# A two-block transformer kernel on one core: bias table in parts, one strip split on VectorE, a maximum moved ahead of a gate, and a reordered first stage

## The reference, cut to what matters

```python
def reference(x, ...):
    x = first_block(...)          # norm, projections, windowed attention, spatial gating, conv-gated MLP
    return second_block(x, ...)   # 16 meta tokens put in front

# second_block, after norm and projection
y_mla = _mla(...) * silu(g_mla)   # 8 latent heads, softmax over all 528 positions
y_na  = _na(...)  * silu(g_na)    # 16 heads, neighbourhood attention on an 8 x 64 grid + meta keys
h_res = h_res + concat([y_mla, y_na]) @ w_out
return h_res[:, 16:]
# in _na: s_win = q.k * scale + bias[head, dr, dc];  s_meta = q.k_meta * scale + meta_bias[head]
```

## Time and profile before

| | |
|---|---|
| median of 3 runs | 1300.63 us (1299.13 to 1302.37) |
| profiled execution | 1300.07 us |
| its span | 1298.3 us |
| TensorE busy | 98% of the span |
| VectorE, ScalarE, GpSimd busy | 57%, 36%, 48% |
| granted TensorE clock, mean | 0.998 of full speed |

### The profile page before, as it was taken

How to read it: one execution, slowest core, us unless ns; L and a number is a source line. 1 busy time by engine, 2 the same in 40 slices (tenths; PEclk the granted TensorE clock), 3 DMA queues, 4 the chain that set the end, 5 groups by cost and what they waited for, 6 DMA issues and landing times.

```text
span 1298.3 us, 20151 instructions
## 1 busy us (share of the span) xinstructions
PE 1267.6 (98%) x6814; PEld 1037.6 (80%) x6814; DVE 735.0 (57%) x1402; ACT 470.8 (36%) x1027; POOL 624.4 (48%) x416
## 2 busy tenths in 40 slices
PE   7999999999999999999999999999999999999998
PEld 6877777778788888888888878888878788888877
DVE  5236777567874545442324778778643556666532
ACT  3233333412422222221113556566402454555521
POOL 5433233237454444345563153443347777777712
PEclk9999999999999999999999999999999999999999
DMA  6412222233242333323333211111133322222213
GB/s 180 119 46 85 81 65 72 60 98 97 75 120 84 95 95 96 98 78 101 98 97 98 66 50 49 48 32 49 49 96 93 94 78 78 77 77 77 65 33 98
DMA packets 196755, 105.42 MB, mean 81 GB/s; under 512 B 19174, under 2 KB 194636, under 8 KB 196700
## 3 DMA queue, kind: packets, MB, share of 16 engines
q1 hardware_dynamic: 196252, 104.00, 28.3%
q0 software_dynamic: 432, 0.69, 0.3%
q10 hardware_dynamic: 16, 0.00, 0.0%
HBM read 102.57 MB, written 2.10 MB: 81 GB/s over the span
## 4 chain that ended last, share of the span: by engine, by line
PE 84%; DVE 5%; POOL 4%; issue 2%; ACT 2%; DMA 2%; SPq 1%; DVEq 0%; ACTq 0%; POOLq 0%
PE ps L387 20%; PE ps L388 19%; PE ps L389 19%; PE ps L418 7%; POOL w_low L366 2%; POOL nb L760 2%; PE ps L1397 1%; PE ps L1428 1%; PE ps L1157 1%; PE ps L1408 1%; DVE w_high L361 1%; PE ps L400 1%; PE ps L401 1%; PE ps L404 1%; DMA x_tok<-in_x_dram 1%
## 5 line engine op out<-in xcount | busy, mean ns | idle before, releaser
L366 POOL TENSOR_TENSOR w_low<-w_raw,w_high 128x1024 fp32r<-128x1024 f32 x180 | 440.3, 2448 | 475.2 <-DVE w_high L361 470.0
L387 PE MATMUL ps<-h_high,w_high 128*128 128x512 f32 x816 | 331.2, 406 | 0.9 <-DVE h_low L527 0.4
L388 PE MATMUL ps<-h_low,w_high 128*128 128x512 f32 x816 | 322.3, 395 | 0.0
L389 PE MATMUL ps<-h_high,w_low 128*128 128x512 f32 x816 | 321.1, 394 | 0.0
L361 DVE CAST w_high<-w_raw 128x1024 fp32r<-128x1024 f32 x183 | 150.1, 822 | 115.6 <-DMA w_raw<-in_w_in_dram 44.0
L387 PEld LDWEIGHTS ps<-h_high,w_high 128*128 128x128 f32 x816 | 153.3, 188 | 40.4 <-issue 5.4
L389 PEld LDWEIGHTS ps<-h_high,w_low 128*128 128x128 f32 x816 | 153.4, 188 | 34.9
L388 PEld LDWEIGHTS ps<-h_low,w_high 128*128 128x128 f32 x816 | 153.3, 188 | 33.8 <-issue 2.6
L1713 ACT ACTIVATE z<-ps,cv 128x512 f32<-128x512 f32 x42 | 32.7, 778 | 147.4 <-PE ps L389 147.4
L2315 DVE SCALAR_TENSOR_TENSOR z<-ps,cv,z 128x511 f32<-128x511 f32 x42 | 31.4, 749 | 91.9 <-ACT z L1713 91.9
L389 PE MATMUL ps<-m_high,w_low 128*128 128x512 f32 x176 | 69.4, 395 | 0.0
(11 more groups left out here) (374 smaller groups left out, 2382.2 us busy)
## 6 DMA issues: line engine op xcount, KB each, us to landing
w_raw<-in_w_in_dram SPq DMA_DIRECT2D x150, 256.0 KB, 3.2
w_raw<-in_w_up_dram SPq DMA_DIRECT2D x88, 256.0 KB, 3.1
w_raw<-in_w_out_dram SPq DMA_DIRECT2D x44, 256.0 KB, 3.0
w_raw<-in_w_down_dram SPq DMA_DIRECT2D x32, 256.0 KB, 3.0
w_raw<-in_w_down_dram SPq DMA_DIRECT2D x16, 192.0 KB, 2.6
rel<-in_rel_bias_dram SPq DMA_DIRECT2D x16, 192.0 KB, 3.0
x_tok<-in_x_dram SPq DMA_DIRECT2D x4, 512.0 KB, 5.5
w_raw<-in_w_ob_dram SPq DMA_DIRECT2D x8, 256.0 KB, 2.9
```

What stands on the lines that cost most here:

```text
L366: pool.tensor_tensor(w_low[:, n % RING, :], w_raw[:, n % RAW, :], w_high[:, n % RING, :].bitcast(F32), ALU.subtract).then_inc(low_made, 1)
L387: pe.matmul(acc, wh, mh, start=first and k == 0, stop=False)
L388: pe.matmul(acc, wh, ml, start=False, stop=False)
L389: done = pe.matmul(acc, wl, mh, start=False, stop=last and k == tiles - 1)
```

## The change

Five things are changed.

1. First stage. SP issues token tile 0 first, then the identity, then tile 2; ACT issues tiles 1 and 3 and after them `rows_m`. Tiles 1 and 3 are squared on VectorE, 0 and 2 on ACT; ACT scales tile 3 and keeps raw tile 0. TensorE's turns of the scaled tiles are put in an order that needs fewer banks at first. VectorE's order is: gain copy, square 1, scale 0 and 1, square 3, scale 2, keep raw 1, `make_high(0)`.
2. First strip. TensorE waits for strip 0's high half only, multiplies by it for all k, and follows with the low weights three k later; the six k are done before the raw turns of tiles 2 and 3, as they were.
3. Latent attention. `m_top(0, 0, 0)` is ahead of `m_gate(0, 0)` and `make_high(N_MLA + 4)`; TensorE's wait for the split of the rotary key is inside the first scores, ahead of the products that use it.
4. Pair 1's bias table in three parts on GpSimd: head 0 between `make_low(N_NA + 6)` and `make_low(N_NA + 7)`; head 1 after `make_low(N_NA + 8)`; the four meta copies after `low_of(.., 1)`.
5. Last stage. Strip `N_ON + 4` is split on VectorE (`split_here`); tile 2's second half of the output is stored by ACT.

```diff
 @block.sync
-            sp.dma_start(ident[:], c_ident).then_inc(s["ident_in"], 16)
-            for t in range(4):
-                sp.dma_start(x_tok[:, t, :], ...)
+            sp.dma_start(x_tok[:, 0, :], x[0, 0:P, :]).then_inc(s["x_in"], 16)
+            sp.dma_start(ident[:], c_ident).then_inc(s["ident_in"], 16)
+            sp.dma_start(x_tok[:, 2, :], x[0, 2 * P:3 * P, :]).then_inc(s["x_rest_in"], 16)
...
                 for t in range(4):
+                    if (half, t) == (1, 2):
+                        continue
 @block.gpsimd
-            def bias_table(i, c):
+            def bias_table(i, c, hs=(0, 1), meta=True):
...
             def pair(i, c, more=True):
                 if more:
                     ahead = N_NA + 4 * (c + 2)
                     if c:
                         bias_table(i, c + 1)
                     squares_low(i, c + 1, 0)
                     make_low(pool, ahead, i * 8)
+                    if c == 0:
+                        bias_table(i, 1, (1,), False)
                 if c:
                     y_parts(i, c - 1)
                 if more:
                     squares_low(i, c + 1, 1)
-                    if c == 0:
-                        bias_table(i, c + 1)
                     make_low(pool, ahead + 1, i * 8)
                     low_of(i, c + 1, 0)
                     low_of(i, c + 1, 1)
+                    if c == 0:
+                        bias_table(i, 1, ())
                     make_low(pool, ahead + 2, i * 8)
                     make_low(pool, ahead + 3, i * 8)
...
-            for n in range(N_NA + 5, N_NA + 8):
+            for n in range(N_NA + 5, N_NA + 7):
                 make_low(pool, n)
+            bias_table(0, 1, (0,), False)
+            make_low(pool, N_NA + 7)
             pair(0, 0)
...
-            for n in range(N_ON + 4, N_END):
+            for n in range(N_ON + 5, N_END):
 @block.tensor
+            pe.wait_ge(s["norm_scaled"], 2)
+            for k in range(4):
+                row_turn(0, k)
+            pe.wait_ge(s["x_ready"], 1)
+            for k in range(4, 6):
+                row_turn(0, k)
+            pe.wait_ge(s["norm_scaled"], 4)
+            for k in range(6):
+                row_turn(1, k)
             pe.wait_ge(s["x_ready"], 2)
-            ... (all turns, after both x_ready)
-            pe.wait_ge(low_made, 1)
-            product(pe, ps[:, 0, :], N_SGU, 0, P, KT, hx, ks=(0, 6), ready=("norm_low", 0))
+            for k in range(6, KT):
+                row_turn(0, k)
+                row_turn(1, k)
+            pe.wait_ge(high_made, 1)
+            for k in range(6 + 3):
+                if k < 6:
+                    pe.wait_ge(s["norm_low"], k + 1)
+                    wh, (mh, ml) = w_high[:, 0, k * P:(k + 1) * P], hx(k)
+                    pe.matmul(ps[:, 0, :], wh, mh, start=k == 0, stop=False)
+                    pe.matmul(ps[:, 0, :], wh, ml, start=False, stop=False)
+                if k >= 3:
+                    if k == 3:
+                        pe.wait_ge(low_made, 1)
+                    pe.matmul(ps[:, 0, :], w_low[:, 0, (k - 3) * P:(k - 2) * P], hx(k - 3)[0], start=False, stop=False)
...
+                    if first and b == 0:
+                        pe.wait_ge(s["pe_split"], 2)
...
-            pe.wait_ge(s["pe_split"], 2)
             m_scores(0, 0, 0, first=True)
 @block.scalar
+            act.dma_start(x_tok[:, 1, :], x[0, P:2 * P, :]).then_inc(s["x_in"], 16)
+            act.dma_start(x_tok[:, 3, :], x[0, 3 * P:S, :]).then_inc(s["x_rest_in"], 16)
             act.dma_start(rows_m[:], mix_norm[0].rearrange("(c p) -> c p", p=P)).then_inc(s["consts_in"], 16)
...
+                if half == 0:
+                    raw_copy(0, 4, 2)
+            act.wait_ge(s["norm_root"], 4)
+            act.activation(xh_tok[:, 3, :], x_tok[:, 3, :], ACT.Copy, scale=x_root[:, 3:4]).then_inc(s["norm_scaled"], 1)
...
+            act.wait_ge(s["out_left"], 6)
+            act.dma_start(out[0]...[2][:, :, 512:D], y_tok[:, 2, 512:D]).then_inc(s["out_stored"], 16)
 @block.vector
-            keep_x(0, 4, 2)
+            square_token(1, s["x_in"])
+            scaled_tokens(0, (0, 1))
+            square_token(3, s["x_rest_in"])
+            scaled_tokens(1, (2,))
             keep_x(1, 6, 3)
-            scaled_tokens(0)
-            scaled_tokens(1)
             make_high(dve, 0)
...
                 m_top(i, c, 0)
+                if c == 0:
+                    m_gate(0, 0)
+                    make_high(dve, N_MLA + 4)
...
             m_place_v(0, 0)
-            m_gate(0, 0)
-            make_high(dve, N_MLA + 4)
             head_then_odd(0, 0)
...
-                make_high(dve, N_ON + m + 4)
+                if m == 0:
+                    split_here(dve, N_ON + 4)
+                else:
+                    make_high(dve, N_ON + m + 4)
```

More of the change, by code:

```diff
@@ L749, in bias_table @@
                 z_ = c % 2
-                for h in range(2):
+                for h in hs:
                     for o, m, r, n in ((NA_OFF[1] + META, 8, 8, 2), (NA_OFF[1] + META + P, P + 8, P + 8, 2),
@@ L761, in bias_table @@
                             .then_inc(s["nb_ready"], 1)
-                for o in (0, NA_OFF[1], NA_OFF[2] + 2 * P, NA_OFF[3] + P):
+                for o in (0, NA_OFF[1], NA_OFF[2] + 2 * P, NA_OFF[3] + P) if meta else ():
                     pool.tensor_copy(nb[:, z_, :, o:o + META],
@@ L846, in _, with row_turn @@
             raw_turn(1, 6)
-            pe.wait_ge(s["x_ready"], 2)
[L848 to L854, removed]
-            pe.wait_ge(low_made, 1)
-            product(pe, ps[:, 0, :], N_SGU, 0, P, KT, hx, ks=(0, 6), ready=("norm_low", 0))
+            def row_turn(half, k):
+                for t in (2 * half, 2 * half + 1):
+                    mm = pe.transpose(ps[:, k, t * P:(t + 1) * P], xh_tok[:, t, k * P:(k + 1) * P], ident[:])
+                if half:
+                    mm.then_inc(s["in_turned"], 1)
+            pe.wait_ge(s["norm_scaled"], 2)
[7 more added lines that the diff above has]
+                row_turn(1, k)
+            pe.wait_ge(s["x_ready"], 2)
+            for k in range(6, KT):
[12 more added lines that the diff above has]
+                    pe.matmul(ps[:, 0, :], w_low[:, 0, (k - 3) * P:(k - 2) * P], hx(k - 3)[0], start=False, stop=False)
             pe.wait_ge(s["x_rest_in"], 32)
@@ L1579, in _, with raw_copy @@
             act.wait_ge(s["ones_set"], 2)
+            def raw_copy(t, bank, count):
+                act.wait_ge(s["in_turned"], count)
+                act.activation(x_t[:, :, t * P:(t + 1) * P],
+                               ps[:, bank:bank + 2, :].rearrange("p b (k q) -> p (b k) q", q=P), ACT.Copy)\
+                    .then_inc(s["x_ready"], 1)
             for half in range(2):
+                t = 2 * half
                 act.wait_ge(s[("x_in", "x_rest_in")[half]], 32)
-                for t in (2 * half, 2 * half + 1):
-                    act.activation(xh_tok[:, t, :], x_tok[:, t, :], ACT.Square, accum_out=x_sum[:, t:t + 1])\
-                        .then_inc(s["norm_sq"], 1)
+                act.activation(xh_tok[:, t, :], x_tok[:, t, :], ACT.Square, accum_out=x_sum[:, t:t + 1])\
+                    .then_inc(s["norm_sq"], 1)
                 act.wait_ge(s["norm_sq"], 2 * half + 2)
@@ L2086, in _ @@
                 act.activation(y_tok[:, t, 512:D], ps[:, OUT_BANK[t], :], ACT.Copy).then_inc(s["out_left"], 1)
+            act.wait_ge(s["out_left"], 6)
+            act.dma_start(out[0].rearrange("(r g c) d -> g c r d", g=CG, c=16)[2][:, :, 512:D], y_tok[:, 2, 512:D])\
+                .then_inc(s["out_stored"], 16)
         @block.vector
@@ L2093, in _, with scaled_tokens @@
             dve.tensor_copy(mix_gain[:], ps[:, 4, 0:KT]).then_inc(s["cols_ready"], 1)
-            def scaled_tokens(half):
+            def scaled_tokens(half, ts):
                 dve.wait_ge(s["norm_root"], 2 * half + 2)
-                for t in (2 * half, 2 * half + 1):
+                for t in ts:
                     dve.tensor_scalar(xh_tok[:, t, :], x_tok[:, t, :], x_root[:, t:t + 1], None, ALU.mult)\
@@ L2104, in keep_x, with square_token @@
                                 ps[:, bank:bank + 2, :].rearrange("p b (k q) -> p (b k) q", q=P)).then_inc(s["x_ready"], 1)
-            keep_x(0, 4, 2)
+            def square_token(t, ready):
+                dve.wait_ge(ready, 32)
+                dve.tensor_tensor_reduce(xh_tok[:, t, :], x_tok[:, t, :], x_tok[:, t, :], 1.0, 0.0, ALU.mult, ALU.add,
+                                         x_sum[:, t:t + 1]).then_inc(s["norm_sq"], 1)
+            square_token(1, s["x_in"])
+            scaled_tokens(0, (0, 1))
+            square_token(3, s["x_rest_in"])
+            scaled_tokens(1, (2,))
             keep_x(1, 6, 3)
-            scaled_tokens(0)
-            scaled_tokens(1)
             make_high(dve, 0)
```

1 line of the change is left out of this document (removed).

## The result

The changed kernel took 1303.12 us (median of 20 runs, 1301.54 to 1304.47), the kernel before 1300.07 in as many runs beside it: ratio 1.0019, 95% interval 1.0012 to 1.0026, or +2.5 us. That is slower by something real, and inside the 0.3% that the prediction called no change. 1303.1 had been predicted.

A forecast was written before the change was run, and what follows sets the result against it. TensorE was taken as the bound, busy 98% of the span, so only its idle places could give time back. The terms +1.1 + 0 + 3.5 - 1.2 - 0.4 = +3.0 on 1300.07 gave 1303.1 us, range 1296.0 to 1305.6.

The forecast's parts named there:

- `rows_m` (R = 9.7, chain of 8.2, +0.4): First stage: `rows_m` lands at R, VectorE's chain takes 8.2 us from there, so the first `h_low` starts 0.4 later.
- Starting by the high half alone is worth nothing.: First product: no gain from starting without the low half, since `h_low` and not `w_low` comes last.
- The 0.7 of the lag: First product: low weights three k behind leave three more matmuls after the sixth `h_low`, costing 0.7 us.
- Latent attention 0: Second scores' 1.8 us wait goes but is waited a few instructions later: gain 0, from -0.2 to +0.2.
- one of the signs: Latent attention: no wait for `me` at the second scores, but some 1.8 us at L1217 to L1220 or the turn before.
- the squares that the prediction named: Latent attention: GpSimd's `m_squares`, behind `make_low(N_MLA + 4)`, were to be what TensorE waits for next.
- The table: +3.5 from 1.9 (table's end) and 1.6 (exclusion): Pair 1's bias table: later end costs 1.9 net, filled GpSimd gaps delaying VectorE 1.6; range +1.9 to +4.3.
- The 21.6 us chain: From pair 1's table end through strip `N_NA + 10` to TensorE going on: 21.6 us, with no free time.
- The exclusion: Pair 0: GpSimd instructions in the filled gaps hold up VectorE's `probs` and `normed`; 1.6 us, between nothing and 2.4.
- Last stage: -1.2 and -0.4: VectorE's low half of strip `N_ON + 4` saves 1.2 of 1.71 us; last store on its own queue saves 0.4.
- The table in the gaps does what it says: Rival, pair 1's table: TensorE regains 2.7 and 0.69, later end costs nothing; -3.9 in all, 1296.2 us; chance 0.14.
- `rows_m` isn't held up: Rival, first stage: last tokens at 11.0 set the pace, stage -1.4, whole +0.5, 1300.6 us; chance 0.12.

The follow-up runs named there:

- rows_first: Changed kernel with `rows_m` issued first on ACT's queue, ahead of both token tiles: ratio 0.9993 to the kernel before.
- repaired_low_in_order: Changed kernel with `rows_m` first and meta copies ahead of the low halves, but the first product in the old order: 0.9947 to the kernel before.
- repaired_gate_ahead: Changed kernel with `rows_m` first and meta copies ahead of the low halves, but latent attention as before: 0.9942 to the kernel before.
- meta_late: Kernel before with only pair 1's four meta copies moved behind both `low_of`, the table's additions left in place: ratio 1.0037 to the kernel before.
- meta_early: Changed kernel with the meta copies right behind head 1's part and the squares, ahead of the low half and both `low_of`: 1298.12 us, 0.9974 to the kernel before.
- tables_only: Kernel before with only the bias-table part of the change: 1303.76 us against 1301.64, ratio 1.0022.
- first_stage_only: Kernel before with only items 1 and 2 of the change: 1301.40 us against 1301.64, ratio 0.9999.
- repaired_block: Changed kernel with `rows_m` first, but pair 1's table in one block ahead of both `low_of`: ratio 0.9985 to the kernel before.

## Why the prediction was right, point by point

- **`rows_m` (R = 9.7, chain of 8.2, +0.4).** The middle of 8.3 to 11.0 was a choice, and that it came out at 9.52, with the turn at 9.65, is luck. The chain took 7.75: turn and copy are 0.37 and not 0.5, and an instruction right behind another starts up to 0.1 before that one's time is over. So `h_low` is 0.1 earlier than before, not 0.4 later. By the Trainium skill's rule ("DMA: Bandwidth & Descriptors", "Why a DMA increments its semaphore by 16 and not by 1", with the slow engines of its measured facts) R would have been near its upper end of 11. It landed half a microsecond ahead of the last tokens (9.52 and 9.99), so no slow engine held it behind them. `rows_first` confirms that R sets this stage.
- **"Starting by the high half alone is worth nothing."** This step was wrong. It said that `h_low` and not `w_low` comes last, but the trace of before has this for the product's start:

```profile
18.75 0.50 PE L387 MATMUL ps<-h_high,w_high 128*128 128x512 f32 x1 [0.32 <-POOL w_low L366]
```

  In the changed kernel strip 0 is cast later and its `w_low` is there only at 19.95; in the old order the product would have started then, 1.6 later than it did. The 0.7 of the lag was sized rightly against the kernel before (from the first `h_low` to the product's end 6.24, before 5.58). Its sign as a part was wrong, as `repaired_low_in_order` shows. The stage gave +0.6 in place of +1.1.
- **Latent attention 0.** Right in size, by the rows and by `repaired_gate_ahead`. The wait moved to the turn, as one of the signs said, but what ended it is a scaling on VectorE that took 2.62 beside the low half on GpSimd; the squares that the prediction named are waited for right behind it, for 0.16. It left out the clock, which took 0.9 here; that it doesn't show in the sum is owed to the wait at 980 us, and is luck.
- **The table: +3.5 from 1.9 (table's end) and 1.6 (exclusion).** The mechanism was right and shown by `meta_late` and `meta_early`. The 21.6 us chain held to the tenth (it is 22.1 in `meta_late`). The exclusion was sized too high: less the 0.4 by which this trace runs late at pair 0, the table ends 2.6 late, so 1.9 + 0.7. The `probs` scalings took 1.14 and not 2.62, and the five `normed` 3.18, most of it hidden. What was missing is the clock: +1.6 behind the wait. Together 4.2, against 4.1 from mark to mark (`tables_only` has 3.2): two errors of opposite sign.
- **Last stage: -1.2 and -0.4.** The split gave 1.17. The store gave 0: SP's last issue does start 0.03 behind VectorE's copy instead of 0.4, and the store then takes 3.9 us to the end of the span instead of 3.4.
- **The sum.** +0.6 + 0 + 4.1 - 1.2 + 0 = +3.5 in the trace (the span grew by 3.4) against +3.0 predicted and +2.5 measured by the ratio. That the sum came so near is in part luck: the first stage and the exclusion were put too high and the clock was left out.
- **The rivals.** "The table in the gaps does what it says" named as its condition that strip `N_NA + 10` lands by 1036.5. It missed by 3 us, and once `meta_early` made the table early, the gain was there (0.9974, -3.4 on the kernel before, where the rival had -3.9). "`rows_m` isn't held up" was worth -2.8 and not -1.4, because it overlooked that the tokens land earlier too and that the high halves need not wait for `w_low`.

## What to carry to other kernels

When work is split to fill an engine's gaps, look at the last increment that others wait for, however small its instruction: four copies of 0.2 us held up a 21.6 us chain here, and their place alone was worth 5.9 us, half clock behind the stall included. The same holds for a queue: the small transfer that the first instruction needs goes first. And a part that loses may be a good one behind a late signal.

## What was not expected of the hardware

- The clock of TensorE fell to 1.2 GHz for 3 to 7 us behind waits of 1.74 (latent attention, changed), 1.78 (`meta_late`), 2.57 (`first_stage_only`), 2.69 (`repaired_block`) and 3.46 us (the changed kernel), and stayed full behind others of 1.73 (`repaired_low_in_order`), 2.69 (before) and 3.49 us (`meta_late`). The length of the wait alone doesn't tell; a stall left in the plan has to be priced with what the clock may add, 1.6 us in the changed kernel. The Trainium skill ("TensorE: Matmul & The Clock Gate", "What's actually happening") says that how many matmuls run slow at a start differs from one execution of a kernel to the next. No kernel has two kept traces here, but kernels with the same instructions around the latent attention's wait of 1.73 to 1.74 differ in the same way: seven of nine fell.
- One VectorE instruction was held for 5 us by a run of GpSimd's instructions (5.71 instead of 0.75). The Trainium skill ("SBUF — State Buffer", "Who interferes with whom") has the one that comes second blocked for the whole of the other's instruction; here it was more than one. Two traces with the same spacing of the starts to 0.1 us differ in it. Whether this is why the kernels with the block spread over several us (`repaired_block` 1295.6 to 1301.3) was not tried. The clock has a share in it: that kernel's runs have a mean granted clock of 0.999 at 1295.6 us and of 0.994 at 1301.25.
